# A two-layer transformer on one core: layers written out, shared splits moved, norm by halves, index keys and forget columns from row products, last expert step tile by tile

## The chip, the cores and the metric

The kernel runs on one core of a Trainium2 chip. The metric is the device time of one execution in microseconds, the median of several runs. Engines: PE (TensorE matmul; PEld is its weight load), DVE (VectorE), ACT (ScalarE), POOL (GpSimd) and SP (SyncE), which only issues DMAs here.

## The reference, cut to what matters

Two layers, 256 tokens (two tiles of 128), width 1024, float32.

```
for layer in range(2):
    fox_qkv, fox_f, dsa_qkv, idx_q, idx_k, idx_w, c_q, c_kv, k_r, band_qkv = split(x @ w_in[layer])
    mixed = concat([fox_group(fox_qkv, fox_f, b_forget[layer]),     # decay = cumsum(log_sigmoid(f + b))
                    dsa_group(dsa_qkv, idx_q, idx_k, idx_w, t5),     # keeps the 64 best keys by index score
                    mla_group(c_q, c_kv, k_r, ...),                  # rms_norm of c_q, c_kv, then w_uq, w_ukv
                    band_group(band_qkv, chunk_rel_bias[layer])])
    x = layer_norm(ALPHA * x + mixed @ w_out[layer])
    scores = sigmoid(x @ w_router); sel = top_k(scores + bias, 8)
    ffn = sum over 64 experts e of gate[e] * (silu(x @ gu[e]) * ...) @ down[e]  +  shared expert
    x = layer_norm(ALPHA * x + ffn)
```

The index score is `sum_h relu(iq_h . ik) * iw_h`: 8 heads of 32 against one key of 32.

## The kernel before, in words

A weight enters a ring `raw` of six slots by a DMA of SP, about 1 MB a piece. Exact float32 products are made of three fp32r products: ACT casts the weight to a high part, POOL (in the first half of a layer) or DVE (later) subtracts to get the low part, and PE adds `xh*wh + xl*wh + xh*wl`. The order on each engine is written out by hand, and semaphores join the engines. One loop over the layers (`Fori(0, DEPTH)`, lines 498, 630, 709, 1119 and 1455) runs on every engine; in it lies a loop of 15 passes over the experts and a 16th pass written apart (`step(NIT - 1, True)`).

Stages of a layer, with the names that the change touches:

- **Projection.** `transpose_x` turns x, ACT and DVE split it (L1130, L1459). Then PE runs jobs 0 to 13, each a product with one unit of `w_in` (48 matmuls of 256 columns; L694). Job 0 is the index query. Job 1 (`columns(job(1)[0:IDM...])`, line 737) makes the index key transposed, 24 matmuls with only 32 stationary columns, and ACT copies it into four bands of `ik_t` (L1205). Job 2 makes index key, index weight and `c_q` by rows. `index_dots(1)` follows, ACT applies relu (`relus(1)`, L1161), and DVE runs `index_scores(1)` (L1475, L1478), which frees the way for `mark_top` (L1488, L1490: rounds of max and replace) and for the scaling of the latents `c_q` and `c_kv` (L1510, L1511). PE meanwhile runs jobs 3, 4 and 5; job 5 (line 743) is 24 matmuls with 4 stationary columns for the forget logits. Then PE waits for `latent_ready` (line 747), transposes the latents (L749 to L751), runs job 6 and the small products L758 to L769.
- **Attention.** For each group and tile: `query_key`, `biased_max` on DVE, `exps` on ACT, `normalize` on DVE (L1590), `transpose_probs` on PE (L797), `values` (L810). Jobs 7 to 13 and the output product (`out_part`, L826) fill PE between them. Between `biased_max("fox", 0)` and `normalize("fox", 0)` DVE does `mark_top(0, 4)` and `keep_top(0)` (L1488 to L1495).
- **Norm 1.** After `mixed_low("dsa", 1)` DVE makes the low parts of both halves of the shared expert's weight (`shared_lo`, L1633) and then runs `layer_norm` for tile 0 and tile 1 (L1437 to L1451). ACT makes their high parts (`shared_hi`, L1318) after `mixed_high("dsa", 1)`.
- **Router.** PE transposes x (L679), runs quarter 0 of the shared gate and up product (L910 to L912), the router product (L956), four matmuls with zeros that open the output banks (L960), quarters 1 to 3 between the small products that rank the experts, and then the shared down product (L933), which needs `a_hi`, `a_lo` from DVE (L1710, L1701, L1703). These need the silu of the shared gate (`silu_dense(0)`, L1353), which stands behind the copies of the first rows on ACT.
- **Experts.** Each pass takes a dense expert A, a gathered one B and a pair C1, C2. The end of a pass: B down (L1059), A down (`dense_down`, L933), scatter of B (L947), pair down (L1085), scatter of C (L947). In the 16th pass `tile0_done` and `moe_done` rise once a tile, after the last scatter into it.
- **Norm 2.** `layer_norm` on the whole tile of 1024 columns: one add of the residual (L1437), two `bn_stats` (L1441), then the rest. `x_next` starts the next layer.

SP reloads the ring for the next layer (L515) as the 16th pass frees the slots: slots 0, 1 and 2 first, then 3, 4, 5.

## Time and profile before

| what | us |
|---|---|
| median of 3 runs (lowest, highest) | 1816.24 (1814.83, 1820.38) |
| the profiled execution: its own time | 1813.22 |
| the profiled execution: its span | 1811.4 |
| PE busy | 1712.4 (95%) |
| DVE, ACT, POOL busy | 986.2, 768.0, 227.4 |
| mean granted clock | 0.977 |
| DMA | 509.26 MB, mean 281 GB/s |

The span is one execution of the program; its own time is the device time of the same execution. A busy PE is not PE at its peak, since matmuls overlap: a row of one matmul shows 0.28 us where the next begins 0.12 us later. Times in the rows count from the span's start. Layer 0 lies at 0 to 906, layer 1 at 906 to 1811; what one row shows for layer 1 stands in layer 0 about 890.9 us earlier.

### The profile page before, as it was taken

How to read it: one execution, taken by the hardware profiler on the slowest of the kernel's cores; microseconds unless marked ns; L12 is line 12 of the kernel's file. 1: busy time of each engine (PE TensorE's matmuls, PEld its weight loads, DVE VectorE, ACT ScalarE, POOL GpSimd, SP SyncE). 2: the span in 40 equal slices, each digit the busy share in tenths (PEclk: the TensorE clock that was granted, in tenths of full speed). 3: DMA queues.
4: the chain of work that ended last, by engine and by line, in shares of the span. 5: the costliest groups of instructions: out<-in, count | busy, mean ns of one | idle time of the engine just before them, and what ended most of it. 6: DMA issues, size and time to landing. Idle time of an engine off the chain costs nothing.

```text
span 1811.4 us, 29520 instructions
## 1 busy us (share of the span) xinstructions
PE 1712.4 (95%) x10302; PEld 1302.3 (72%) x10302; DVE 986.2 (54%) x1441; ACT 768.0 (42%) x1020; POOL 227.4 (13%) x160
## 2 busy tenths in 40 slices
PE   7798999999999999999979988999999999999996
PEld 6687766777777777767677876777776777777774
DVE  2746455555555555555457555555555555555554
ACT  4464333443444434444346634443444444334331
POOL 6380000000000000000144700000000000000000
PEclk8898999999999999999989989999999999999998
DMA  8232699889899989888853228888888898888983
GB/s 286 85 130 65 222 337 328 331 332 333 334 338 332 335 333 335 333 330 320 290 173 114 97 70 325 330 334 336 336 332 335 317 327 336 330 322 334 330 322 116
DMA packets 136091, 509.26 MB, mean 281 GB/s; under 512 B 11588, under 2 KB 50920, under 8 KB 102760
## 3 DMA queue, kind: packets, MB, share of 16 engines
q1 hardware_dynamic: 122288, 467.77, 70.0%
q0 software_dynamic: 9792, 35.66, 6.0%
q10 hardware_dynamic: 3960, 5.17, 0.9%
q8 instruction: 30, 0.49, 0.1%
q14 instruction: 21, 0.17, 0.0%
HBM read 505.14 MB, written 3.41 MB: 281 GB/s over the span
## 4 chain that ended last, share of the span: by engine, by line
PE 81%; DVE 7%; DMA 4%; ACT 3%; DVEq 2%; issue 2%; ACTq 0%; SPq 0%; PEldq 0%
PE ps L1044 11%; PE ps L933 10%; PE ps L1018 10%; PE ps L910 7%; PE ps L947 7%; PE ps L911 7%; PE ps L912 7%; PE ps L1085 6%; PE ps L694 5%; PE ps L1059 5%; DMA raw<-in_w_exp_down_dram 2%; PE ps L940 2%; PE ps L826 1%; DVE o_lo L1745 1%; DMA raw<-in_w_exp_gu_dram 1%
## 5 line engine op out<-in xcount | busy, mean ns | idle before, releaser
L1717 DVE TENSOR_TENSOR raw_r<-raw,w_hi 128x2048 fp32r<-128x2048 f32 x192 | 439.9, 2292 | 397.6 <-ACT w_hi L1365 397.6
L1365 ACT CAST w_hi<-raw 128x2048 fp32r<-128x2048 f32 x192 | 365.7, 1906 | 286.7 <-DMA raw<-in_w_exp_down_dram 175.5
L910 PE MATMUL ps<-x_hi,w_hi 128*128 128x256 f32 x1088 | 311.4, 286 | 1.8 <-DVE x_lo L1643 1.8
L911 PE MATMUL ps<-x_lo,w_hi 128*128 128x256 f32 x1088 | 306.9, 282 | 0.0
L912 PE MATMUL ps<-x_hi,raw_r 128*128 128x256 f32 x1088 | 306.2, 281 | 0.0
L1044 PE MATMUL ps<-raw,xc 128*64 128x512 f32 x1024 | 233.8, 598 | 0.0
L910 PEld LDWEIGHTS ps<-x_hi,w_hi 128*128 128x128 f32 x1088 | 206.6, 190 | 31.4 <-issue 30.1
L911 PEld LDWEIGHTS ps<-x_lo,w_hi 128*128 128x128 f32 x1088 | 207.9, 191 | 1.5
L912 PEld LDWEIGHTS ps<-x_hi,raw_r 128*128 128x128 f32 x1088 | 206.7, 190 | 0.0
L657 POOL DMA_INDIRECT xg_b<-x_by_token,token_b x32 | 30.1, 940 | 1248.2 <-DVE token_c L1696 1248.2
L1044 PEld LDWEIGHTS ps<-raw,xc 128*64 128x64 f32 x1024 | 67.8, 136 | 119.4 <-issue 115.0
L1745 DVE TENSOR_TENSOR o_lo<-ps,o_hi 128x512 fp32r<-128x512 f32 x128 | 87.8, 688 | 58.2 <-ACT o_hi L1415 24.3
L933 PE MATMUL ps<-w_hi,a_hi 128*128 128x512 f32 x272 | 112.2, 413 | 6.3 <-DVE a_lo L1703 6.3
L1085 PE MATMUL ps<-raw,at_c 128*64 128x512 f32 x512 | 116.9, 598 | 0.0
L933 PE MATMUL ps<-w_hi,a_lo 128*128 128x512 f32 x272 | 107.9, 397 | 0.0
L1018 PE MATMUL ps<-w_hi,xb_hi 128*128 128x512 f32 x256 | 102.5, 401 | 1.3 <-DVE xb_lo L1725 1.3
L933 PE MATMUL ps<-raw_r,a_hi 128*128 128x512 f32 x256 | 101.0, 395 | 0.0
L1018 PE MATMUL ps<-raw_r,xb_hi 128*128 128x512 f32 x256 | 100.5, 392 | 0.0
L1018 PE MATMUL ps<-w_hi,xb_lo 128*128 128x512 f32 x256 | 99.8, 390 | 0.0
L1085 PEld LDWEIGHTS ps<-raw,at_c 128*64 128x64 f32 x512 | 33.9, 136 | 66.6 <-issue 66.6
L636 POOL TENSOR_TENSOR raw_r<-raw,w_hi_odd 128x1024 fp32r<-128x1024 f32 (+1 forms) x28 | 68.6, 2471 | 63.5 <-ACT w_hi_odd L1126 63.5
L694 PE MATMUL ps<-x_hi,raw_r 128*128 128x256 f32 (+2 forms) x256 | 74.9, 293 | 0.0
(314 smaller groups left out, 2962.3 us busy)
## 6 DMA issues: line engine op xcount, KB each, us to landing
raw<-in_w_exp_gu_dram SPq DMA_DIRECT2D x256, 1024.0 KB, 6.4
raw<-in_w_exp_down_dram SPq DMA_DIRECT2D x128, 1024.0 KB, 7.5
raw<-in_w_in_dram SPq DMA_DIRECT2D x22, 1024.0 KB, 5.8
raw<-in_w_out_dram SPq DMA_DIRECT2D x8, 1024.0 KB, 5.1
row_b<-gates_by_rank SPq DMA_DIRECT2D x30, 256.0 KB, 5.7
row_c<-gates_by_rank SPq DMA_DIRECT2D x60, 128.0 KB, 5.3
raw<-in_w_sh_gu_dram SPq DMA_DIRECT2D x4, 1024.0 KB, 5.4
row_a<-gates_by_rank SPq DMA_DIRECT2D x32, 128.0 KB, 8.1
```

The lines of the kernel that those rows point to most:

```text
L694: last = nc.tensor.matmul(o, a, b, start=(c == 0 and i == 0), stop=(c == KC - 1 and i == 2))
L910: nc.tensor.matmul(o, h, x_hi[:, c, :], start=(first and i == 0), stop=False, skip_group_check=True)
L911: nc.tensor.matmul(o, h, x_lo[:, c, :], start=False, stop=False, skip_group_check=True)
L912: last = nc.tensor.matmul(o, l, x_hi[:, c, :], start=False, stop=(final and i == 3), skip_group_check=True)
L933: last = nc.tensor.matmul(ps[:, 4 + 2 * t + half, :], lhs, rhs, start=False, stop=False, skip_group_check=True)
L947: last = nc.tensor.matmul(ps[:, 4 + 2 * t + half, :], place[:, t * P:(t + 1) * P], part[:, half * 512:(half + 1) * 512], start=False, stop ...
L1018: last = nc.tensor.matmul(ps[:, 2, :], a[:, c, :], b[:, i, :], start=(c == 0 and k == 0), stop=(c == KC - 1 and k == 2))
L1044: last = nc.tensor.matmul(ps[HALF * h:HALF * (h + 1), 3, :], xc[:, c, HALF * h:HALF * (h + 1)], piece_slot(j % RING, u)[:, i, :], start=(c ...
L1085: last = nc.tensor.matmul(ps[HALF * h:HALF * (h + 1), 2 + half, :], at_c[:, c, HALF * h:HALF * (h + 1)], piece_slot(j % RING, 2)[:, c, hal ...
L1365: nc.scalar.copy(w_hi[CAST[j] % 3][:], raw[:, j % RING, 0:UNIT_F]).then_inc(hi_done, 1)
L1717: nc.vector.tensor_tensor(raw_r[:, s, 0:UNIT_F], raw[:, s, 0:UNIT_F], w_hi[CAST[j] % 3][:], ALU.subtract)\
L1745: nc.vector.tensor_tensor(o_lo[:, part], ps[:, bank + half, :], o_hi[:, part], ALU.subtract)\
```

## The change

`for layer in range(DEPTH)` takes the place of all five layer loops, so each layer has its own code; the loop over the experts stays. The rest, cut to its core:

```diff
 # PE: projection. Job 1 gone, later jobs one number lower; job 5 gone
-columns(job(1)[0:IDM, 0:SEQ], layer, 1, 0, IDM, True).then_inc(job_ps, 1)
-project_rows(2, 1)
-pe.wait_ge(job_sb, done(layer, job_sb, 2))
+project_rows(1, 1)
+o = job(2)
+rows(o, layer, 2, (0,))
+pe.wait_ge(ik_rows_sb, done(layer, ik_rows_sb, 1))
+for t in range(NT):
+    last = nc.tensor.transpose(ps[:, 4, t * P:(t + 1) * P], ik_rows[:, t]..., ident[:])
+last.then_inc(ik_ps, 1)
+rows(o, layer, 2, (1,)).then_inc(job_ps, 1)
+pe.wait_ge(ik_sb, done(layer, ik_sb, 1))
 index_dots(1)
-project_rows(3, 2)
-project_rows(4, 3)
-columns(job(5)[0:NH, 0:SEQ], layer, 3, GW, NH, False).then_inc(job_ps, 1)
+tile_rows(job(3), layer, 3, 0).then_inc(job_ps, 1)      # 24 matmuls of 260 columns each
+tile_rows(job(4), layer, 3, 1).then_inc(job_ps, 1)
 ...
+    last = nc.tensor.transpose(ps[0:NH, 5, SEQ + t * P:...], f_tok[:, t, :], ident[:])   # after the latents' transposes
 # ACT: projection
-for r in range(4): last = nc.scalar.copy(ik_t[IDM * r:IDM * (r + 1), :], o[0:IDM, 0:SEQ])
+nc.scalar.copy(ik_rows[:], o[:, :, 0:IDM].unsqueeze(2).to_broadcast([P, NT, 4, IDM])).then_inc(ik_rows_sb, 1)
 split_pre(3)
 nc.scalar.mul(iw[:], ...)
-relus(1)
 nc.scalar.copy(cq_tok[:], ...)
+act.wait_ge(ik_ps, done(layer, ik_ps, 1))
+nc.scalar.copy(ik_t[:], ps[:, 4, 0:SEQ]).then_inc(ik_sb, 1)
 ... squares of cq_tok ...
 o = bank(2)                 # was bank(3)
 split_pre(4)
+relus(1)
 nc.scalar.copy(ckv_tok[:], o).then_inc(job_sb, 1)
 ...
+for t in range(NT):         # jobs 3 and 4; the root of the rms stands inside, at t == 0
+    o = bank(3 + t)
+    if t == NT - 1: split_pre(5)
+    nc.scalar.copy(v_tok["fox"][:, t, :], o[:, 0:GW])
+    nc.scalar.copy(f_tok[:, t, :], o[:, GW:GW + NH]).then_inc(job_sb, 1)
+    if t == 0: wait var_ready; Sqrt of rms
 relus(0)
 # DVE: attention and norm 1
 biased_max("fox", 0)
-mark_top(0, 4)
-keep_top(0)
-normalize("fox", 0)
+mark_top(0, 2)
+normalize("fox", 0)
+mark_top(0, 2)
+keep_top(0)
 ...
 mixed_low("dsa", 0)
+shared_lo(0)
 mixed_low("dsa", 1)
-shared_lo(0); shared_lo(1); layer_norm(tile 0); layer_norm(tile 1)
+layer_norm(tile 0); shared_lo(1); layer_norm(tile 1)
 # ACT: shared_hi(0) before probs_out("dsa", 1), shared_hi(1) after it, both before mixed_high("dsa", 1);
 # silu_dense(0) right after the copies of mask_t, waiting for shared_gate_ps (quarter 1 done)
 # PE: the four matmuls with zeros from before quarter 1 to behind the matmul that makes ranked_ps
 def layer_norm(layer, t, bank, signal, roots, ready):
+    for half, (s, n) in enumerate(ready):
+        dve.wait_ge(s, n)
+        scalar_tensor_tensor(part, part, ALPHA, ps[:, bank + half, :], mult, add)
+        dve.drain()
+        bn_stats(stats[:, t, half, :], part)
 # PE: the 16th pass, behind B down and the transposes of a_c
+pair_down()
+add_b()
+for t in range(NT):
+    for half in range(2):
+        last = dense_down(t, *weights(AD), (half,))
+        if t == 0 and half == 0: pe.wait_ge(c_out_sb, ...)
+        scatter(place_c, t, (half,)).then_inc((tile0_done, moe_done)[t], 1)
 # ACT, 16th pass: waits for b_added before it reads C's output
 # SP: before a layer's load into slot k it waits for the last use in the order (0, 1, 2, 4, 5, 3)
```

## Rows read from the trace of the kernel before

**Rows 1.** The profile's page, part 1: busy time, share of the span, instructions.
```profile
PE 1712.4 (95%) x10302; PEld 1302.3 (72%) x10302; DVE 986.2 (54%) x1441; ACT 768.0 (42%) x1020; POOL 227.4 (13%) x160
```

**Rows 2.** Busy time by stage: stretch, length, engines' busy us, granted clock, DMA share, GB/s.
```profile
219.80:886.00 666.20, 657.95 (x3728) 478.58 (x3728) 365.37 (x478) 271.68 (x291) 28.10 (x30) 1.00 0.89 330
886.00:919.30 33.30, 22.41 (x98) 14.42 (x94) 18.13 (x27) 8.48 (x14) 6.72 (x4) 0.83 0.73 238
```

**Rows 3.** Waits of PE, whole span: us in total, times, longest us.
```profile
PE ps L679 <- DVE x_tok L1451: 23.3, 6, 5.0
PE ps L749 <- DVE ckv_tok L1511: 9.4, 2, 8.7
PE ps L797 <- DVE probs L1590: 7.7, 4, 3.0
```

**Rows 4.** Timeline of ACT, layer 1: start us, us, engine, line, operation.
```profile
936.45 2.02 ACT L1126 CAST w_hi_odd<-raw 128x1040 fp32r<-128x1040 f32 x2 [4.22 <-PE ps L694]
938.45 2.04 ACT L1161 ACTIVATE ps<-ps 128x512 f32<-128x512 f32 x4
943.48 2.00 ACT L1126 CAST w_hi_even<-raw 128x1024 fp32r<-128x1024 f32 x2 [1.51 <-PE ps L694]
```

**Rows 5.** Timeline of DVE at the latents' scaling, layers 0 and 1.
```profile
55.24 1.89 DVE L1510 TENSOR_SCALAR cq_tok<-cq_tok,rms 128x192 f32<-128x192 f32 x1
57.05 2.36 DVE L1511 TENSOR_SCALAR ckv_tok<-ckv_tok,rms 128x128 f32<-128x128 f32 x1
...
952.25 0.32 DVE L1510 TENSOR_SCALAR cq_tok<-cq_tok,rms 128x192 f32<-128x192 f32 x1
```

**Rows 6.** Chain that ended last, layers 0 and 1: start us, us, piece.
```profile
61.44 7.42 PE ps L694 x48
...
919.33 17.10 PE ps L694 x120
...
954.12 5.63 PE ps L694 x48
```

**Rows 7.** Timelines of POOL, DVE and ACT, layer 1, around fox.
```profile
981.75 5.13 POOL L636 TENSOR_TENSOR raw_r<-raw,w_hi_even 128x1024 fp32r<-128x1024 f32 x2 [4.38 <-ACT w_hi_even L1126]
...
981.91 2.73 DVE L1590 TENSOR_TENSOR probs<-probs,row_inv 128x512 f32<-128x512 f32 x1
...
990.41 1.16 ACT L1268 COPY mk_t<-ps 32x256 f32<-32x256 f32 x4
```

**Rows 8.** Timeline of DVE, layer 1, before norm 1.
```profile
1051.63 4.50 DVE L1633 TENSOR_TENSOR raw_r<-raw,w_hi 128x2048 fp32r<-128x2048 f32 x2 [1.38 <-ACT w_hi L1318]
1056.04 1.22 DVE L1437 SCALAR_TENSOR_TENSOR x_tok<-x_tok,ps 128x1024 f32<-128x1024 f32 x1
```

**Rows 9.** Timelines of PE and ACT, layer 1, the router.
```profile
1079.04 1.17 PE L960 MATMUL ps<-x_hi,zeros 128*128 128x512 f32 x4
...
1092.52 1.28 ACT L1353 ACT_TABLE_LOAD   x1 [0.61 <-PE ps L912]
1093.82 0.60 ACT L1353 ACTIVATE silu<-ps 128x512 f32<-128x512 f32 x1
...
1096.61 0.79 PE L933 MATMUL ps<-w_hi,a_hi 128*128 128x512 f32 x1 [3.19 <-DVE a_lo L1703]
```

**Rows 10.** Timelines of PE and DVE at layer 0's end.
```profile
898.74 3.65 PE L1085 MATMUL ps<-raw,at_c 128*64 128x512 f32 x16
903.92 0.47 PE L947 MATMUL ps<-o_hi,place_c 128*128 128x512 f32 x1 [1.53 <-DVE o_lo L1745]
...
905.20 1.22 DVE L1437 SCALAR_TENSOR_TENSOR x_tok<-x_tok,ps 128x1024 f32<-128x1024 f32 x1 [1.43 <-PE ps L947]
...
915.26 1.28 DVE L1451 SCALAR_TENSOR_TENSOR x_tok<-x_tok,rstd,ln_b 128x1024 f32<-128x1024 f32 x1
```

**Rows 11.** Line 709 (the layer loop) on PE's queue; ACT's timeline at the boundary.
```profile
L709 PEldq COMPARE_BRANCH  x2: 74/2994/5913, 904.0 to 1794.5; - x2
...
916.60 1.28 ACT L1130 ACT_TABLE_LOAD   x1 [2.44 <-issue]
```

More of the change, by code:

```diff
@@ L629, in _ @@
                                pattern=[[-1, NH], [0, P]], channel_multiplier=1).then_inc(consts_built, 1)
-            with pool.Fori(0, DEPTH) as layer:
+            for layer in range(DEPTH):
                 def split_lo(k, before):
@@ L882, in _ @@
                 values("mla", 0)
[L883 removed]
+                pe.wait_ge(job_sb, done(layer, job_sb, 13))
                 out_part(0, FOX_C + BAND_C, (2, 3), first=True)
@@ L941, in gathered_t, with scatter @@
                     last.then_inc(signal, 1)
-                def scatter(place, t):
-                    for half in range(2):
+                def scatter(place, t, halves=range(2)):
+                    for half in halves:
                         for part in (o_hi, o_lo):
@@ L958, in _ @@
                 last.then_inc(router_ps, 1)
-                for b in range(2 * NT):
-                    nc.tensor.matmul(ps[:, 4 + b, :], zeros[:], x_hi[:, 0:2, :], start=True, stop=False, skip_group_check=True)
                 shared_gate_up(1)
@@ L1102, in step @@
-                    if not final:
+                        pe.wait_ge(place_c_ready, done(layer, place_c_ready, it + 1))
+                        pe.wait_ge(c_out_sb, done(layer, c_out_sb, it * 2 + 2))
+                        for t in range(NT):
+                            scatter(place_c, t)
                         pe.wait_ge(xb_lo_sb, done(layer, xb_lo_sb, it * 2 + 4))
@@ L1118, in _ @@
             act.dma_start(t5_dram, t5_row[:]).then_inc(t5_stored, 16)
-            with act.Fori(0, DEPTH) as layer:
+            for layer in range(DEPTH):
                 def split_pre(k, halves=range(2)):
@@ L1334, in _, with silu_dense @@
                     .then_inc(scores_ready, 1)
+                def silu_dense(n):
+                    act.wait_ge(a_ready, done(layer, a_ready, n))
+                    nc.scalar.activation(silu[:].rearrange("p c t -> p (c t)"), ps[:, 0, :], ACT.Silu).then_inc(silu_a_done, 1)
                 shared_hi(2)
@@ L1454, in _ @@
                 dve.sem_inc(s, START[s])
-            with dve.Fori(0, DEPTH) as layer:
+            for layer in range(DEPTH):
                 for b in range(4):
```

267 lines of the change are left out of this document (139 added, 128 removed).

## The prediction

> **What bounds the kernel now.** I read the page's busy times first: PE is busy for 95% of the span [rows 1]. That is an average, so I went to the busy times by stage. In the expert passes PE works 657.95 of 666.20 us at granted clock 1.00, DVE and ACT about half of that, and the DMA engines are 0.89 busy [rows 2]. The change leaves the 15 looped passes as they are, so 30 of the 32 passes should not move. In the 33.3 us around the layer boundary PE is busy 22.41 us only, at clock 0.83 [rows 2]: there and between the attention and the first pass the time can change. The waits of PE say on whom: on the second norm result (L679, 23.3 us in six waits), on the scaled latents (L749: 9.4 us in two, of which one is 8.7, so the other is 0.7), and on the normalized probabilities (L797: 7.7 us in four, the longest 3.0) [rows 3]. The chain of waits and the engines' timelines give the rest. I price one layer at a time, since the two latents' waits are so different.
>
> **Index keys and forget columns by rows.** What goes: 24 matmuls of job 1 and 24 of job 5. The chain has 120 matmuls in 17.10 us, of which 28 ran at the half rate; the 48 of a later job take 5.63 us, 0.117 us each [rows 6]. So 2.8 + 2.8 = 5.6 us of PE work go from each layer. In their place stand two transposes for the keys and two for the forget columns, about 0.1 us each (0.2 at the half clock), and 4 more columns on 48 matmuls (1.6% of 5.6 us, 0.1). The question is whether PE could use the gain. PE waits for `latent_ready`, and that hangs on this chain: relu of the index dots on ACT, index scores, six rounds of max and replace, scaling, all on DVE.
>
> In layer 1 the chain gets longer at its head. Before, `relus(1)` ran at 938.45, right behind the cast of unit 3 [rows 4], when 120 matmuls had ended. Now job 1 by rows (48) and job 2 (48) stand before the dots, so it is 144 matmuls: 2.8 us later, with the transposes 3.1. And `relus(1)` stands behind `split_pre(4)`, which waits for job 2 and takes 2.00 us where the cast of unit 3 took as much [rows 4]. PE's job 0 ends at 927.8; plus 5.6, 2.8, 0.3, 2.8 gives 939.4 for the end of job 2; plus 2.0 for the cast gives 941.4 against 938.45. So all that follows on DVE is 2.9 us late.
>
> Then comes a second loss. In layer 0 the scaling ran while POOL split unit 5: 1.89 and 2.36 us where the same operation takes 0.32 in layer 1 [rows 5]. Layer 1 escaped because ACT waited for job 5 (until 951.8) before it cast unit 5, and POOL began at 953.0, behind the first scalings. Job 5 is gone, so ACT casts unit 5 as soon as it has the root, as in layer 0. I take layer 0's stretch: the four scalings take 4.6 us from the first's start (55.24 to 59.8) instead of 0.95, less 0.4 because the cast no longer waits for a copy: +3.3. `latent_ready` comes at 953.2 + 2.9 + 3.3 = 959.4, and PE, done with its jobs at about 949, idles 10 us.
>
> Third: behind layer 0's idle of 8.7 us, 48 matmuls took 7.42 us, behind layer 1's 0.7 us 5.63 [rows 3, 6]: +1.8. The transposes before them also run at the half rate: +0.7, and +0.4 for the two new ones. Sum for layer 1: 2.9 + 3.3 + 1.8 + 0.7 + 0.4 = **+9.1 us**. Bounds: 2.2 if the hold and the clock fall away and ACT overlaps something, 10.5 if the hold is layer 0's in full.
>
> In layer 0 the head has slack: DVE is held until 43.5 by the bias tables, and the later `relus(1)` would end at 42.1. The 0.4 us that the hold loses pay the two new transposes: **0** (0 to +1.5). The forget logits now come behind the latents; the decay is then ready near 972 in layer 1, and PE wants it after job 6, near 980: nothing.
>
> The Trainium skill, "SBUF — State Buffer", section "SBUF: two separate sides", calls the port pair that VectorE and GpSimd share an exclusive lock, held for a whole instruction, that bites VectorE operations with two SBUF inputs or in a two-port mode. By that rule the hold comes wherever POOL's split is under way; without it this part would be near +5.
>
> **Rounds after the normalization.** PE waits 3.0 us a layer at L797, for a `normalize` of 2.73 us that began 0.2 us after POOL's split did [rows 3, 7]. Put two rounds of max earlier it starts near 980.1 and ends at 980.8, before POOL's 981.75: PE's wait is gone. But what is late next? `keep_top` falls into POOL's split now and is held till its first half ends (984.2), so `biased_max("fox", 1)` gains only 0.4; ACT's `exps("fox", 1)` follows it, and the copies to `mk_t`, which PE awaits, end at 991.6 now [rows 7], 0.3 before PE reads them. So PE waits there instead: **-0.6 us a layer** (0 to -3.0; I stay at the near end, as ACT's order is fixed).
>
> **Shared splits and norm 1.** Before, 4.50 us of low parts stood before the first norm, which began at 1056.04 [rows 8], though its product had ended at 1048.3. Now DVE is free at 1050.25 (after `mixed_low`). A norm takes 5.7 us (1056.04 to 1061.7); by halves it costs one more start on each of two operations, +0.3. So 1050.3 + 6.0, then 2.25 for the second low part, then 6.0: 1064.6 against 1067.4. DVE binds, not PE's product (ended 1058.2). ACT's two casts of 1.9 us lie in gaps before the probabilities' copies; the first low part lies before `mixed_low("dsa", 1)`, in an idle stretch of 5.3 us. **-2.75 us a layer** (-1.5 to -3.5).
>
> **Router.** The four zero matmuls go from a place where PE was the bound to one where it idled 3.19 us [rows 9]: -0.95, their start to start. `silu_dense(0)` had its table load of 1.28 and its 0.60 us on the way to `gated` [rows 9]; now DVE goes on as soon as its `tokens` end (1093.1), a further -1.3. The idle before L933 shrinks from 3.19 to about 0.9, less the zeros; the first six of its matmuls ran at the half rate (0.43 us apart, not 0.23), so up to -1.2 more. Against this the gathered rows and the DMAs behind `ranked_stored` come only about 1.1 and 1.8 us earlier. The silu's new wait for quarter 1 (ended by 1083) holds the copies of `by_expert` behind it on ACT, but they await PE until 1087 anyway. I take **-2.7 us a layer** (-1.5 to -4).
>
> The Trainium skill, "ScalarE: Activation LUTs", section "What ACT_TABLE_LOAD costs", gives some 2.66 us for a switch with its drain. The row has 1.28, and the silu starts right behind it at 1093.82. By the page this part would be -4.1; the trace decides.
>
> **16th pass and norm 2.** `pair_down` comes first. It needs `at_c`, ready at 892.04, so it starts at 892.15, 0.8 us idle after 891.36. With 3.63 for it, 1.86 for B's scatter: 897.65. ACT and DVE then need 2.2 us for C's output, half hidden by 1.4 us of dense down; tile 0's first half is complete at 900.5, the second at 902.3, and the statistics end near 903.8, where they ended at 907.8: tile 0's norm ends at 907.0. Tile 1 is complete at 906.0, DVE binds: 907.0 + 6.0 = 913.0 against 916.5 (915.26 + 1.28) [rows 10]. **-3.55 us a layer** (-2 to -4.5). Behind ACT's new wait for B's scatter stand only C's copies, and DVE's `o_lo` waits for those. PE's 1.53 us wait for `o_lo` [rows 10] is replaced by one of about 0.9. Queues: SP now asks for slot 3 only after the last down product and for 4 and 5 behind it, at about 906 instead of 897 to 903; three loads of 3.2 us end near 916, and ACT first wants unit 3 at 930.
>
> **Layers written out.** PE's branch back took 5.9 us (904.0 to 910.0) [rows 11], hidden behind the norm of tile 0 that ended at 910.9. With tile 0 at 907.0 it would delay only its transposes, so the jump is worth little by itself. ACT had its branch and a table load of 1.28 us on the path of `x_hi` [rows 11]; layer 1's middle, which has none, goes from the norm to the first low part 0.5 us faster: **-0.5, once**. Register operations before waits go too: under 1 us, taken as 0. In the looped passes a wait still needs a register: 0 (bounds below).
>
> **Sum.** 9.1 - 2 x (0.6 + 2.75 + 2.7 + 3.55) - 0.5 = 9.1 - 19.2 - 0.5 = -10.6 us. On the profiled execution's 1813.2 us that is 1802.6. The median shown is 3.0 us above that execution, so I state 1805.6.
>
> **Rivals.**
> 1. *The latents cost little.* Layer 1's late head is absorbed, the hold and the half clock don't come: +2.2 instead of +9.1, so 1816.2 - 17.5 = 1798.7, or less if the earlier normalization reaches PE in full (-4.8): 1794. For it: POOL's start moves with ACT's, and 0.7 us were enough to escape. Against: layer 0 shows hold and clock under just this order.
> 2. *The gains at the norms stay small.* `pair_down` waits for its last piece, issued at 884.8 and landed near 889.8, 2.3 us before the need; and DVE's norm in halves takes longer. Half of the 19.2 us and the full +9.1: -1, so 1815.
> 3. *Slower: the looped passes get longer.* A pass is 43.1 us and the 30 looped passes are untouched in text, but they now exist twice, in a longer program. If the code behind the loop's branch has to be fetched again, as at the layer's branch (5.9 us for PE [rows 11]), even a tenth of that, 0.6 us a pass, is +18: 1816.2 - 10.6 + 18 = 1823.6. It decides from 0.35 us a pass on. Against: PE is idle for only 8 of 666 us in the passes, the inner branch included [rows 2].
>
> **How the numbers follow.** Forecast 0.50 (its own range 1801 to 1811), rival 1 0.28, rival 2 0.12, rival 3 0.10. What a measurement here can tell from no change is 0.3%, 5.4 us. Faster by more: 0.47 of the forecast, all of rival 1 and 0.02 of rival 2, 0.77; within: 0.03, 0.10 and 0.02, 0.15; slower: 0.08. The range for 8 in 10 runs from rival 1's low end to the near side of rival 2: 1794 to 1813.
>
> **What would show it.** In the profile after, per step: PE's wait at the latents' transposes in layer 1 (some 10 us for 0.7), the scalings of `cq_tok` there at about 2 us and the job behind them at 7.4; a `normalize("fox", 0)` of 0.7 us and a new PE wait for ACT's `mk_t`; norm 1 starting right after `mixed_low`; no PE wait over 1.5 us before the shared down product; the last norm 3.5 us sooner after B's down product. The prediction is wrong if layer 1's latents are ready within 3 us of their old place, or if a looped pass is not 43.1 us.

## The result, and the profile after

The changed kernel takes 1803.4 us in the median of six runs (1800.4 to 1805.7), the kernel before 1815.5 (1810.1 to 1820.5, six). The ratio is 0.9928, 95% interval 0.9907 to 0.995: faster by 9 to 17 us, by medians 12.1. Forecast were 1805.6 us and 10.6 us less. The profiled execution has a span of 1801.6 us, against 1811.4.

Some words used below. A split is the subtraction that makes the low part of a weight; on POOL it comes in two halves of some 2.4 us each. A hold is the time by which a DVE operation is longer beside a split. Half rate is TensorE at the lower of its two clocks.

I cut both traces at the same matmuls: the first projection, the latents' transposes (L749, now L766), the query matmuls (L758, L779), the probabilities of fox 1 (L797, L818), the first output matmul, the first shared one (L910, L931), the first of B's in a pass (L1018, L1041). Each number is the difference of two start times, in us; only the row from the last output matmul counts from its end.

```
layer, stretch                         before   after  difference  forecast
0  first projection -> latents          43.01   44.46     +1.4        0
0  latents -> query matmuls              8.80    8.71     -0.1        0
0  query matmuls -> fox 1               32.31   31.96     -0.4       -0.6
0  fox 1 -> first output matmul         34.86   36.93     +2.1        0
0  last output matmul -> shared         12.16    9.03     -3.1       -2.75
0  shared -> first expert matmul        35.82   31.10     -4.7       -2.7
0  first pass                           43.96   44.42     +0.5        0
0  14 looped passes                    604.4   604.0      -0.5        0
0  last pass -> layer 1's projection    55.74   51.96     -3.8       -3.55 and -0.5
1  first projection -> latents          33.92   37.90     +4.0       +6.2
1  latents -> query matmuls              6.35    8.84     +2.5       +2.9
1  query matmuls -> fox 1               32.32   31.68     -0.6       -0.6
1  fox 1 -> first output matmul         34.85   34.62     -0.2        0
1  last output matmul -> shared         12.17    9.04     -3.1       -2.75
1  shared -> first expert matmul        35.83   32.70     -3.1       -2.7
1  first pass                           44.39   46.89     +2.5        0
1  14 looped passes                    603.5   604.4      +0.9        0
1  last pass -> end                     57.37   53.75     -3.6       -3.55
```

(The output product itself is 0.15 shorter in each layer.) The page's busy times answer to [rows 1]: 88 matmuls fewer, the share unchanged.

```profile
PE 1703.4 (95%) x10214; PEld 1292.6 (72%) x10214; DVE 989.6 (55%) x1449; ACT 763.3 (42%) x1019; POOL 226.3 (13%) x160
```

By stage, as in [rows 2] (length, then busy us of PE, PEld, DVE, ACT, POOL, granted clock, DMA share, GB/s): layer 0's looped passes; the last pass with the boundary; and in layer 1 the latents, the job behind them, and on to fox 1.

```profile
253.00:859.00 606.00, 599.63 (x3375) 435.45 (x3374) 334.07 (x436) 249.60 (x268) 26.28 (x28) 1.00 0.90 331
859.00:910.58 51.58, 43.91 (x240) 31.29 (x239) 28.27 (x41) 13.94 (x21) 6.80 (x4) 0.95 0.76 257
910.58:948.49 37.91, 26.44 (x227) 25.34 (x227) 22.93 (x46) 17.87 (x39) 24.29 (x10) 0.86 0.65 198
948.49:957.33 8.84, 8.84 (x57) 8.59 (x58) 5.80 (x19) 5.29 (x9) 0.00 (x0) 0.72 0.00 0
957.33:989.01 31.68, 28.89 (x207) 24.41 (x205) 20.65 (x61) 17.62 (x41) 14.13 (x6) 1.00 0.34 107
```

The passes are as full as before: a looped pass is 43.14 to 43.17 us against 43.11 to 43.17. In layer 1's third row PE works 26.4 of 37.9 us, and behind it, at clock 0.72, it is busy all the time and slow. The waits of PE answer to [rows 3]:

```profile
PE ps L766 <- DVE ckv_tok L1555: 20.1, 2, 10.3
PE ps L687 <- DVE x_tok L1495: 16.6, 4, 5.3
PE ps L741 <- DVE drop L1522: 5.1, 2, 4.2
PE ps L818 <- ACT mk_t L1319: 4.6, 2, 2.5
PE ps L818 <- DVE probs L1634: 1.9, 3, 0.9
```

The norms' wait (L679, now L687) lost 6.7 us, the latents' (L749, now L766) gained 10.7; the fox probabilities' went from 7.7 to 1.9, and `mk_t` took their place with 4.6. New is also a wait of 5.1 us in two for the index scores to be read (L741): 4.2 in layer 0, 0.9 in layer 1.

### The profile page after: what moved, and what is told of

The parts are those of the page before. It is cut to its first block, busy times and chain, and to the rows that moved or that the text cites. A ratio compares the mean times of both kernels' runs of the same rounds, so it can differ in the third digit from the quotient of the medians.

```text
span 1801.6 us, 28743 instructions
## 1 busy us (share of the span) xinstructions
PE 1703.4 (95%) x10214; PEld 1292.6 (72%) x10214; DVE 989.6 (55%) x1449; ACT 763.3 (42%) x1019; POOL 226.3 (13%) x160
## 4 chain that ended last, share of the span: by engine, by line
PE 80%; DVE 8%; DMA 5%; ACT 3%; issue 2%; DVEq 2%; ACTq 0%; SPq 0%; PEldq 0%; POOLq 0%
PE ps L1067 11%; PE ps L1041 10%; PE ps L956 9%; PE ps L931 7%; PE ps L970 7%; PE ps L932 7%; PE ps L933 7%; PE ps L1107 6%; PE ps L1082 5%; PE ps L702 4%; DMA raw<-in_w_exp_down_dram 2%; PE ps L963 2%; DVE o_lo L1790 1%; PE ps L847 1%; ACT o_hi L1458 1%
## 5 line engine op out<-in xcount | busy, mean ns | idle before, releaser
L931 PE MATMUL ps<-x_hi,w_hi 128*128 128x256 f32 x1088 | 311.1, 286 | 1.8 <-DVE x_lo L1687 1.8
L931 PEld LDWEIGHTS ps<-x_hi,w_hi 128*128 128x128 f32 x1088 | 206.1, 189 | 31.3 <-issue 30.1
L665 POOL DMA_INDIRECT xg_b<-x_by_token,token_b x32 | 30.5, 952 | 1243.2 <-DVE token_c L1740 1243.2
L1041 PE MATMUL ps<-w_hi,xb_hi 128*128 128x512 f32 x256 | 102.6, 401 | 0.4 <-DVE xb_lo L1770 0.4
L1041 PE MATMUL ps<-raw_r,xb_hi 128*128 128x512 f32 x256 | 100.4, 392 | 0.0
L1041 PE MATMUL ps<-w_hi,xb_lo 128*128 128x512 f32 x256 | 99.8, 390 | 0.0
L1433 ACT ACTIVATE silu_b<-ps 128x256 f32<-128x256 f32 x32 | 12.4, 387 | 140.7 <-PE ps L1041 140.7
```

Source lines behind the costliest of these rows:

```text
L931: nc.tensor.matmul(o, h, x_hi[:, c, :], start=(first and i == 0), stop=False, skip_group_check=True)
L1041: last = nc.tensor.matmul(ps[:, 2, :], a[:, c, :], b[:, i, :], start=(c == 0 and k == 0), stop=(c == KC - 1 and k == 2))
```

## Experiments

Each kernel was timed in rounds with the kernel before on its chip; ratios are to that kernel.

**u_idx**: the changed kernel, with the index keys and the forget columns as column jobs again.

```diff
-                project_rows(1, 1)
-                o = job(2)
...
+                columns(job(1)[0:IDM, 0:SEQ], layer, 1, 0, IDM, True).then_inc(job_ps, 1)
+                project_rows(2, 1)
...
-                tile_rows(job(3), layer, 3, 0).then_inc(job_ps, 1)
-                tile_rows(job(4), layer, 3, 1).then_inc(job_ps, 1)
+                project_rows(3, 2)
+                project_rows(4, 3)
+                columns(job(5)[0:NH, 0:SEQ], layer, 3, GW, NH, False).then_inc(job_ps, 1)
```

> The changed kernel (1803.4 us) with the index keys and the forget columns taken back to their own column jobs (14 jobs, old relu and scaling order); all else stays changed. Theory (the latents cost in layer 1): from layer 1's first projection to the latents' transposes 37.9 us fall to about 32, and the 8.8 us from there to the query matmuls to 6.3, so some 8 us less in layer 1; in layer 0 about 1.4 less before the transposes, and if the wait for the mk_t copies with the half clock behind it hangs on the new order, 2 more behind the first probabilities. Together 1792 to 1796 us. Rival 1 of the prediction (the latents cost little, the job by rows is as good): within 2 us of 1803.4, since the 48 matmuls a layer that come back take 5.6 us of PE where the wait for the latents shrinks by as much.

1796.4 us, ratio 0.9879 (0.9837 to 0.9921). Windows of layer 1, to the latents and behind them:

```profile
919.46:951.45 31.99, 31.66 (x273) 29.77 (x273) 15.55 (x45) 16.46 (x34) 19.11 (x8) 0.96 0.66 202
951.45:957.79 6.34, 6.34 (x55) 6.34 (x56) 3.77 (x10) 6.25 (x14) 4.81 (x2) 1.00 0.53 168
```

PE has more matmuls (273 records for 227) and is through 5.9 us earlier, since it idles for 0.3 us and not for 11.5, and the clock behind it is 1.00. The theory holds for these stretches (8.4 us less in layer 1, 1.6 in layer 0), and rival 1 of the prediction falls. The price of the part, 7 us, is by medians only: four executions lie between 1790.3 and 1808.2, and the interval meets that of the changed kernel at its edge (0.9921 against 0.9907).

The trace is of the slowest of the four, 1808.2 us, and shows where some 8 of its us went. In layer 0 DVE's normalization for band takes 10.84 us, where the same operation takes 0.69, PE waits 8.9 us for it, and the stretch from fox 1 to the first output matmul is 44.8 us (36.9 in the changed kernel):

```profile
114.61 10.84 DVE L1616 TENSOR_TENSOR probs<-probs,row_inv 128x512 f32<-128x512 f32 x1
...
115.63 4.68 POOL L642 TENSOR_TENSOR raw_r<-raw,w_hi_out 128x1024 fp32r<-128x1024 f32 x2
120.24 4.66 POOL L642 TENSOR_TENSOR raw_r<-raw,w_hi_odd 128x1024 fp32r<-128x1024 f32 x2
```

It begins beside a split that started at 110.90 and ends at 125.45, behind the last of the splits that follow without a pause. No other kernel here has a normalization over 3.3 us.

**u_tail, u_norm1, u_router**: the changed kernel with one of the three other parts undone.

```diff
                     if final:
-                        pair_down()
-                        add_b()
                         pe.wait_ge(split_done, cast(layer, split_done, it, AD))
...
-                    layer_norm(layer, t, 4 + 2 * t, x_next, 4 + t, [(s, done(layer, s, half + 1)) for half in range(2)])
+                    layer_norm(layer, t, 4 + 2 * t, x_next, 4 + t, [(s, done(layer, s, 1))] * 2)
```

(In u_tail the four parts of the last pass stand in the order of the other passes again.)

```diff
-                shared_lo(0)
                 mixed_low("dsa", 1)
+                for u in range(2):
+                    shared_lo(u)
```

(u_norm1; ACT's `shared_hi` is behind `mixed_high("dsa", 1)` again, and the norm waits for a whole tile.)

```diff
                 last.then_inc(router_ps, 1)
+                for b in range(2 * NT):
+                    nc.tensor.matmul(ps[:, 4 + b, :], zeros[:], x_hi[:, 0:2, :], start=True, stop=False, skip_group_check=True)
                 shared_gate_up(1)
```

(u_router; `silu_dense(0)` is behind the copies of `row_b` and `row_c` again.)

> The changed kernel with the old order of the 16th pass (dense down, B's scatter, pair_down, C's scatter) and the second norm waiting for a whole tile. Theory: the last pass up to the next layer's first projection gets 3.6 to 3.8 us longer in each layer (52.0 back to 55.7, 53.8 back to 57.4), and the boundary's half-clock stretch, 17.0 us before and 6.8 us after, comes back and adds up to 1.8 in the first job: 1810.5 to 1812.5 us. Rival (the boundary is shorter because the layer's branch and its table load are gone, not because of the order of the pass): only +1 to +3 a layer, 1806 to 1808, with the half-clock stretch still near 7 us.

> The changed kernel with the shared units' high and low parts both back ahead of the first norm, and that norm waiting for a whole tile. Theory (DVE was the bound, 4.5 us of low parts stood ahead of the norm): from the last output matmul to the first shared gate/up matmul 9.0 us go back to about 12.2 in both layers, 1809.7 us. Rival (half of the 3.1 us comes from the norm by halves alone or from fewer register operations): 10.5 us there and 1806.5.

> The changed kernel with the four zero matmuls and the first silu at their old places. The stretch from the first shared matmul to the first expert matmul shrank by 4.7 us in layer 0 and 3.1 in layer 1, but layer 1's first pass got 2.5 us longer (0.5 in layer 0). Theory A (the third piece of the first pass is bound by its DMA, so what the router gives in layer 1 is taken back by a wait and the half clock behind it): with the old order the stretch is 4.7 and 3.1 longer, and the first pass 0.5 and 2.5 shorter, 1808.2 us. Theory B (the long first pass of layer 1 is a clock event that has nothing to do with the router): the stretch grows the same, the first pass stays at 46.9, 1811 us.

u_tail: 1811.1 us, ratio 0.9977 (0.996 to 0.9994). The last pass to the next projection is 56.1 and 57.8 us (52.0 and 53.8): +4.1 twice. The gain is the order of the pass with the norm by halves, which this run undoes together, and not the layer's branch. The second half of the theory fails: the first job of layer 1 has only 6 matmuls at half rate, fewer than the changed kernel. u_norm1: 1810.0, ratio 0.9967 (0.9945 to 0.999), 12.7 us from the output to the shared product in both layers (9.0), as the bound of DVE has it (12.2 before, plus 0.24 for each of two norms by halves). Its DVE, layer 1:

```profile
1058.76 4.49 DVE L1678 TENSOR_TENSOR raw_r<-raw,w_hi 128x2048 fp32r<-128x2048 f32 x2 [1.38 <-ACT w_hi L1359]
1063.16 0.68 DVE L1483 SCALAR_TENSOR_TENSOR x_tok<-x_tok,ps 128x512 f32<-128x512 f32 x1
```

u_router: 1807.9, ratio 0.9951 (0.993 to 0.9972), which overlaps that of the changed kernel, so that the 4.5 us are by medians. The stretch grew to 35.8 and 35.3 us, but layer 1's first pass stayed long, 46.8: my theory A (the gain is taken back there) is wrong as stated. Theory B has the first pass right (46.9), but the stretch grew by 4.7 and 2.6 only, and 1811 was not reached. The first pass was 43.9 to 47.8 us over all kernels here, whatever order the router had; ACT waits some 7.6 us for the first down piece in both profiles, which is a lead and not a cause shown. ACT's cast of it, layer 1, in the changed kernel:

```profile
1116.27 1.91 ACT L1406 CAST w_hi<-raw 128x2048 fp32r<-128x2048 f32 x1 [7.67 <-DMA raw<-in_w_exp_down_dram]
```

and in u_router:

```profile
1121.85 1.91 ACT L1404 CAST w_hi<-raw 128x2048 fp32r<-128x2048 f32 x1 [7.52 <-DMA raw<-in_w_exp_down_dram]
```

Stretch and first pass together are 79.8 to 82.1 us in the six layers with the old router and 75.5 to 80.4 in the 22 with the new one. What of the spread is the DMA's and what is the clock's stays open.

**only_loop**: the kernel before, with the layers written out and nothing else (on SP one line that served its loop, `lower_ap_dma`, goes too).

```diff
-            with pe.Fori(0, DEPTH) as layer:
+            for layer in range(DEPTH):
```

(The same on each of the five engines.)

> The kernel before with the two layers written out, nothing else (the loop over the passes stays). Theory (the branch and the table load of ACT are all that goes): 0.5 us less on the path at the layer boundary, up to 2 if the half-clock stretch there shortens; a looped pass stays at 43.1 to 43.2 us: 1813.5 to 1815.5. Rival 3 of the prediction (the longer program makes the loop's branch dearer): passes of 43.5 us or more, 1826 or more. Rival (the branch was most of the boundary's gain): the last pass up to the first projection of layer 1 falls from 55.7 to 53 or less, 1812.5.

1810.05 us (10 runs), ratio 0.9967 (0.9955 to 0.9978): 6.5 us less, where every expectation had 0.5 to 3. The looped passes didn't lengthen (43.29 and 43.11 us), so rival 3 of the prediction falls. The last pass to the projection is 55.3 for 55.7: the 0.5 of the boundary is right. Another 2.9 came in the attention: 30.9 and 30.9 us from the query matmuls to fox 1, for 32.3 and 32.3. DVE and POOL in layer 1:

```profile
978.88 0.69 DVE L1589 TENSOR_TENSOR probs<-probs,row_inv 128x512 f32<-128x512 f32 x1
...
980.64 4.76 POOL L635 TENSOR_TENSOR raw_r<-raw,w_hi_even 128x1024 fp32r<-128x1024 f32 x2 [6.02 <-ACT w_hi_even L1125]
```

Before, this normalization began at 981.91 and POOL's split at 981.75 [rows 7], so it was late by 0.16 us and held for 2.0. Counted from the first query matmul of fox, that is 7.87 us; now it is 7.52, in both layers, and 7.70 would have been early enough. DVE's small pauses ahead of a wait (0.25 and 0.17 us by its timeline, "issue") are gone; that the loop's registers made them fits, but no row names them. In this trace another thing helps: PE's job ahead (48 matmuls) ran partly at half rate, 7.48 us for 5.90, so ACT's cast and POOL's split came 1.7 us later than before, and even the old normalization would have been ahead. That the 0.35 us are enough alone is shown by u_max below. Another 2.0 and 1.5 us lie ahead of the latents, and there TensorE's rate differs: of the first job's matmuls 13 and 16 were spaced 0.21 us (half rate), for 30 and 28 before, and the others 0.12. Whether the edit brings that or this execution had it, one profile doesn't tell. The profiled execution as a whole is 3.7 us shorter, since the first pass and the looped passes of layer 0 are 1.8 and 1.6 longer; of the 6.5 us by medians only the 2.9 around fox and the 0.5 of the boundary have a place that is shown.

**u_max**: the changed kernel, with `normalize("fox", 0)` behind all four rounds and `keep_top(0)`. **keep_late**: the changed kernel, with `keep_top(0)` moved behind the normalization of fox 1.

```diff
-                mark_top(0, 2)
-                normalize("fox", 0)
-                mark_top(0, 2)
+                mark_top(0, 4)
                 keep_top(0)
+                normalize("fox", 0)
```

```diff
-                keep_top(0)
                 biased_max("fox", 1)
                 normalize("fox", 1)
+                keep_top(0)
```

> The changed kernel with normalize(fox,0) back behind all four rounds of max and keep_top(0). Theory of the prediction (the early normalization takes 3.0 us of PE's wait away and 2.1 to 2.5 come back at mk_t): the stretch from the query matmuls to fox 1's transposes goes from 31.7 to 32.3 in layer 1, 0.6 us a layer, 1804.6 us. Rival (the held normalization and the held keep_top are two forms of one wait on POOL's split, and without it the old order is the better by what keep_top loses): 0 to 1 us less, 1802.4 to 1803.4.

> The changed kernel with keep_top(0) behind normalize(fox,1), nothing else. Theory (keep_top, held by POOL for 1.8 us, delays the maximum of fox 1, ACT's exponentials and with them the copies to mk_t that PE awaits): PE's wait of 2.5 and 2.1 us for mk_t falls to under 1 us, the stretch from the query matmuls to the transposes of fox 1 goes from 32.0 and 31.7 to about 30.3, and layer 0's half clock stretch behind the wait goes: 1799 to 1801 us. Rival (POOL's lock then falls on biased_max(fox,1) or on normalize(fox,1) instead, which take as long): nothing, 1803.4.

u_max: 1797.0 us (five runs, 1796.6 to 1808.7), ratio 0.9924 (0.9897 to 0.9951): the interval doesn't part it from the changed kernel, but the trace does. Layer 1's window to fox 1, then the timelines of DVE and POOL with the normalization and the split:

```profile
955.36:985.40 30.04, 28.79 (x206) 24.43 (x205) 18.79 (x61) 17.59 (x40) 14.44 (x6) 1.00 0.34 106
```

```profile
977.41 0.69 DVE L1634 TENSOR_TENSOR probs<-probs,row_inv 128x512 f32<-128x512 f32 x1
...
977.67 5.05 POOL L644 TENSOR_TENSOR raw_r<-raw,w_hi_even 128x1024 fp32r<-128x1024 f32 x2 [4.54 <-ACT w_hi_even L1164]
```

The expectation and its rival (1802.4 to 1804.6) both missed it. With the layers written out the old order escapes POOL by itself, by 0.26 us (0.18 in layer 0), and is 1.6 to 1.9 us shorter than the new one, which puts `keep_top` under the split.

That price hangs on the rate of PE's job ahead. Six layers of the kernels with the new order here have that job in 5.9 to 6.0 us; the split then starts 22.3 us behind the query matmuls, `keep_top` takes 2.0 us, and the stretch is 31.6 to 32.0. In five others (u_router, lat_first, layer 0 of u_tail) the job took 7.4 to 7.5 us, the split starts at 23.8, `keep_top` takes 0.23, and the stretch is 30.8 to 30.9, as in only_loop with the old order. So the slower job gives the shorter stretch, and as far as these traces go the orders differ only where the job runs at full rate. (Layer 1 of u_idx and split5_late stand apart with 34.4 to 34.9: DVE was held earlier there, at the scan.)

keep_late has the early normalization and a `keep_top` behind the split: 1798.5 us, ratio 0.9902 (0.9882 to 0.9922), the stretch 29.9 and 29.6 us, and PE's wait for `mk_t` 0.5 and 0. Its theory holds.

**lat_first**: the changed kernel, with sums, root and scalings of the latents behind one round of max instead of six. The last two rounds and `keep_top(1)` go behind the decay scan. **lat_keep**: lat_first and keep_late together.

```diff
                 index_scores(1)
-                mark_top(1, 4)
                 dve.wait_ge(sums_ready, done(layer, sums_ready, 1))
...
-                mark_top(1, 2)
+                mark_top(1, 1)
                 dve.wait_ge(root_ready, done(layer, root_ready, 1))
...
                 last.then_inc(latent_ready, 1)
+                mark_top(1, 3)
                 index_scores(0)
...
-                keep_top(1)
                 dve.wait_ge(f_log_ready, done(layer, f_log_ready, 1))
                 nc.vector.tensor_tensor_scan(decay[:], f_abs[:], f_neg[:], 0.0, ALU.add, ALU.subtract).then_inc(decay_ready, 1)
+                mark_top(1, 2)
+                keep_top(1)
```

> The changed kernel with the latents' sums, root and scalings moved ahead: behind one round of max instead of six (the other rounds follow: three before index_scores(0), two before the decay scan, two behind it). Theory (the cost of the new order in both layers is that PE waits for the scaling and then runs at half clock): in layer 1 the index scores end at 937.6 and the scalings would end near 940 instead of 948.4, right behind PE's last index dots (938.2), so PE's wait of 10.3 us falls to about 2 and the half clock behind it (2.5 us) goes; in layer 0 the wait of 9.8 falls to about 2 likewise. Start to latents 36.5 and 30 us (44.5 and 37.9), latents to query matmuls 6.4 (8.7 and 8.8): 20 us less, near 1783. Rival A (DVE is the bound a step later: the rounds only move, and rope, fox bias and the first maxima come late by what PE gains): PE waits some 5 us a layer before the fox probabilities, gain 8 to 10, near 1794. Rival B (POOL's split of unit 5 holds the scalings or the rounds wherever they are): the latents come 3.3 later than above, near 1790.

> As the one with the latents ahead, and keep_top(0) behind normalize(fox,1) as well. Theory: the two waits are apart, so both gains add: PE's wait for the copies to mk_t (2.1 to 2.5 us a layer) falls by the 1.8 us that POOL holds keep_top, so 2 to 4 us under the kernel with the latents ahead alone. Rival: with PE earlier, DVE is late everywhere before the fox maxima and keep_top is no longer under POOL's split: within 1 us of the other.

lat_first: 1792.9 us, ratio 0.9874 (0.9855 to 0.9892): half of what its theory said. PE's wait fell from 9.8 and 10.3 to 5.5 and 6.1 us only. lat_keep: 1789.2, ratio 0.9852 (0.9834 to 0.987), 3.7 less again, as said by number. The step isn't shown: in lat_first's profile both layers have the slower job, `keep_top(0)` is not held (0.23 us) and PE doesn't wait for `mk_t` at all. DVE and POOL of lat_keep, layer 1:

```profile
933.40 2.47 DVE L1553 TENSOR_SCALAR cq_tok<-cq_tok,rms 128x192 f32<-128x192 f32 x1
935.79 2.36 DVE L1554 TENSOR_SCALAR ckv_tok<-ckv_tok,rms 128x128 f32<-128x128 f32 x1
...
933.41 4.66 POOL L644 TENSOR_TENSOR raw_r<-raw,w_hi_odd 128x1024 fp32r<-128x1024 f32 x2 [4.01 <-ACT w_hi_odd L1164]
```

The same root releases ACT's cast, ACT's first half releases POOL, and POOL starts 0.01 us behind the first scaling: 4.8 us for the two operations instead of 0.6. That is rival B, and most of the missing half: with the hold gone (best, below) the two waits are 1.3 and 1.8 us.

**split5_late**: the changed kernel, with ACT's cast of unit 5 behind the forget gates' `f_z`, so that POOL starts on it later. **best**: that and lat_keep. **best2**: lat_keep, with the cast right behind `relus(0)`.

```diff
                     o = bank(3 + t)
-                    if t == NT - 1:
-                        split_pre(5)
...
                 nc.scalar.activation(f_z[:], o, ACT.Identity, bias=b_f[:]).then_inc(f_read, 1)
+                split_pre(5)
```

(split5_late and best.)

```diff
                 relus(0)
+                split_pre(5)
                 act.wait_ge(latent_ps, done(layer, latent_ps, 1))
```

(best2.)

> The changed kernel with ACT's cast of unit 5 moved from ahead of the second copy of the forget job to behind the forget gates' first two operations (before their exponential), so that POOL's low part of unit 5 starts after the latents are scaled. Theory (POOL's split holds the first two scalings for 3.3 us): the scalings of cq_tok and ckv_tok take 0.32 and 0.28 us instead of 1.4 and 2.4, the latents are ready 3.0 to 3.3 us earlier in layer 1 (37.9 to 34.7) and 3.5 to 4.0 earlier in layer 0 (44.5 to 40.8), and PE's two waits of 9.8 and 10.3 us shrink by as much; the half clock behind them stays: 1796 to 1798 us. Rival A (project_t(6) or ACT's own chain is late by the move): the stretch from the query matmuls grows by 2 us a layer, 1801. Rival B (the long scalings have another cause than POOL): no change, 1803.4.

> The latents ahead, keep_top(0) behind normalize(fox,1), and ACT's cast of unit 5 behind the forget gates' first two operations. Theory: what the kernel with the first two edits (1789.2 us) still waits for at the latents is POOL's hold of 4.1 us on the scalings (2.47 and 2.36 us for 0.32 and 0.28); without it PE's waits of 5.5 and 6.1 us shrink to 1.4 and 2.0, and the half clock behind them (10.2 us stretches in both layers) shortens by one or both: 4.1 x 2 plus 1 to 3, so 1778 to 1781 us. Rival (DVE or unit 5's low part becomes late for project_t(6), which PE reaches near 945 us): gain 3 to 5 only, 1785.

> As the kernel with all three edits (1789.9 us), but ACT casts unit 5 right behind relus(0), not behind the forget gates' operations: POOL's low part would then run from about 934.5 to 939.2, beside rounds of max and index scores only, which POOL never lengthened in any run. There the low part fell on the forget gates' addition (2.25 us for 0.27) and the next one but one on two rope operations (2.22 and 2.40 for 0.22), and PE's stretch from the query matmuls to fox 1's transposes was 34.5 and 34.2 us where it is 29.6 to 30.9 without. Theory (the hold isn't lost by moving a split, it lands on DVE's next operation between two SBUF tiles; only beside rounds and PSUM operations it is free): start to latents stays at 36.6 and 29.8, the addition takes 0.27, DVE reaches the rope 2 us earlier and mostly ahead of unit 7's low part, the stretch falls to 30.5 to 32.5: 1783 to 1787 us. Rival (unit 7's low part still meets the rope, as its start hangs on PE's project_t(6) which is no later): the stretch stays over 34, 1788 to 1790.

split5_late: 1804.8 us, ratio 0.9952 (0.9936 to 0.9967), nothing gained, where theory had 1796 to 1798 and rival A 1801. The latents came 2.2 and 2.5 us earlier, and the stretch from the query matmuls to fox 1 grew by 2.9 and 2.8. best: 1789.9, ratio 0.9865 (0.9849 to 0.9882), as lat_keep, and worse than both the theory (1778 to 1781) and its rival (1785). Its DVE and POOL in layer 1 show where it went:

```profile
932.97 0.32 DVE L1552 TENSOR_SCALAR cq_tok<-cq_tok,rms 128x192 f32<-128x192 f32 x1
...
941.25 2.25 DVE L1560 TENSOR_SCALAR f_abs<-f_abs 4x256 f32<-4x256 f32 x1
...
955.64 2.22 DVE L1579 TENSOR_TENSOR mq_tok<-rope_ab 128x64 f32<-128x64 f32 x1
957.79 2.40 DVE L1581 TENSOR_TENSOR mq_tok<-rope_ab 128x64 f32<-128x64 f32 x1
...
938.57 4.78 POOL L644 TENSOR_TENSOR raw_r<-raw,w_hi_odd 128x1024 fp32r<-128x1024 f32 x2 [9.59 <-ACT w_hi_odd L1164]
...
955.17 4.94 POOL L644 TENSOR_TENSOR raw_r<-raw,w_hi_odd 128x1024 fp32r<-128x1024 f32 x2 [5.11 <-ACT w_hi_odd L1164]
```

The scalings are free (0.32 for 2.47), and the hold falls on the forget gates' addition, and by the next but one split on two rope operations that take 0.22 us elsewhere. In best2 unit 5's split runs beside the rounds of max, which it doesn't lengthen: 1783.3 us (1780.7 to 1786.8, six runs), ratio 0.9823 (0.9789 to 0.9857). It beats the changed kernel by 20 us in medians, 19 by the two ratios. Its windows of layer 1, to the latents, behind them, and to fox 1:

```profile
899.69:930.10 30.41, 27.45 (x226) 26.35 (x227) 16.41 (x30) 16.55 (x38) 19.62 (x8) 0.93 0.76 232
930.10:936.67 6.57, 6.57 (x56) 6.52 (x57) 5.52 (x19) 6.08 (x10) 4.78 (x2) 1.00 0.21 72
936.67:970.13 33.46, 30.36 (x206) 25.75 (x204) 27.87 (x77) 17.78 (x42) 14.54 (x6) 0.95 0.30 95
```

In layer 0 the last stretch is 29.9 us, in layer 1 still 33.5: there unit 7's split meets two rope operations (2.37 and 2.38 us). Layer 0 is the theory's (30.5 to 32.5) and better, layer 1 lies between it and the rival's (over 34).

## Why the prediction was right, and where it was not

Of the signs of being wrong that the prediction names, none came: layer 1's latents are 4.0 us later than in the kernel before, past the 3 us, and a looped pass is unchanged. The terms one by one:

**Index keys and forget columns** (forecast 0 and +9.1; measured +1.3 and +6.5; undone, 7.0 in all). The mechanism is the one forecast; the first of its terms, the later relus of layer 1, was sized too large. Chain and scalings in layer 1 answer to [rows 5, 6]:

```profile
910.58 15.31 PE ps L702 x120
...
950.45 7.04 PE ps L702 x48
```

```profile
944.31 1.41 DVE L1554 TENSOR_SCALAR cq_tok<-cq_tok,rms 128x192 f32<-128x192 f32 x1
945.65 2.36 DVE L1555 TENSOR_SCALAR ckv_tok<-ckv_tok,rms 128x128 f32<-128x128 f32 x1
```

The four scalings took 4.1 us from the first's start (944.31 to 948.4), against 0.95 forecast to become 4.6 less 0.4: the hold of 3.3 was 3.2. The job behind the wait took 7.04 for 5.63 (+1.4 for 1.8), the transposes 2.0 for 0.9. What failed is the 2.9 us of the later relus: they end 22.4 us after the first projection (932.95 - 910.58) for 21.2 before (940.49 - 919.33), +1.2, because the first 120 matmuls took 15.3 and not 17.1 us. Nine of them ran at half rate, 28 before. I had carried the boundary's clock over as it stood; the other kernels had 6 (u_tail, u_max) to 20 (u_router, best2) there, and no row says what decides it. In layer 0 I had let the head vanish behind DVE's bias tables. They were themselves held: POOL now splits unit 3 beside them, where before a split met the bias for band, ahead of them.

```profile
40.07 5.81 DVE L1511 TENSOR_TENSOR t_bias<-t_hankel,block 128x256 f32<-128x256 f32 x4
```

It was 1.42 us before, and the index scores start 2.3 us later, at 45.8.

The rule of the Trainium skill that I had put beside this part ("SBUF — State Buffer", section "SBUF: two separate sides": an exclusive lock, for a whole instruction, on VectorE operations with two SBUF inputs or in a two-port mode) agrees with these rows: additions, scalings and the scan were held (0.27 to 2.25, 0.32 to 2.47, 0.67 to 2.29 us); rounds of max and index scores out of PSUM, beside the same splits, kept their 0.43 and 0.48. It does not explain u_idx's 10.84 us: there DVE was held over more than four of POOL's subtractions and not over one, and why it was not let in between them stays open. Without the hold the prediction has this part near +5; its own terms give 9.1 - 3.3 = 5.8.

**Rounds after the normalization** (forecast -0.6 a layer). The stretch did get 0.4 and 0.6 shorter, and what I had named took its place, in layer 1 as in layer 0 [rows 7]:

```profile
977.71 0.69 DVE L1634 TENSOR_TENSOR probs<-probs,row_inv 128x512 f32<-128x512 f32 x1
...
980.09 2.03 DVE L1539 TENSOR_SCALAR drop<-drop 128x128 f32<-128x128 f32 x1
...
987.80 1.16 ACT L1319 COPY mk_t<-ps 32x256 f32<-32x256 f32 x4
```

So the number was met by luck, for the credit is wrong. u_max shows that the written-out layers had already freed the normalization, by 0.35 us of DVE's time; on top of them the moved rounds cost 1.6 to 1.9 us a layer in this stretch, where PE's job ahead runs at full rate. And in layer 0 the wait of 2.5 us has a price that I had left out: the job behind `mk_t` took 7.48 us, at a granted clock of 0.78, where layer 1's took 6.02.

```profile
103.59:111.07 7.48, 7.48 (x52) 7.35 (x52) 0.42 (x1) 3.98 (x7) 7.48 (x4) 0.78 0.03 10
```

**Layers written out** (forecast -0.5, alone -6.5). The step that failed is "register operations before waits: under 1 us, taken as 0". As busy time they are that little. But DVE is 0.35 us sooner at the normalization, which before was 0.16 us behind the split, and u_max shows that this is enough to go first; the stretch to fox 1 is 1.4 to 1.5 us shorter in each layer of only_loop. What makes up the rest of the 6.5 us stays open.

**Norm 1** (forecast -2.75, measured -3.1 in both layers; undone 6.6 in all). DVE binds as said; answers to [rows 8]:

```profile
1046.96 0.68 DVE L1483 SCALAR_TENSOR_TENSOR x_tok<-x_tok,ps 128x512 f32<-128x512 f32 x1
...
1052.82 2.28 DVE L1650 TENSOR_TENSOR raw_r<-raw,w_hi 128x2048 fp32r<-128x2048 f32 x1
...
1059.70 1.28 DVE L1495 SCALAR_TENSOR_TENSOR x_tok<-x_tok,rstd,ln_b 128x1024 f32<-128x1024 f32 x1
```

A norm by halves costs what was forecast: from 1055.02 to 1060.98 is 5.96 us, tile 0's 5.94, where I had 6.0 and the whole one 5.7. The gain is the low part that no longer stands ahead of tile 0's norm.

**Router** (forecast -2.7 a layer; undone 4.5 in all, 2.3 a layer). The stretch itself gained 4.7 and 3.1. The zeros now stand in what is left of the idle time [rows 9], and the table load is ahead of the rows' copies:

```profile
1086.19 1.20 PE L1016 MATMUL ps<-x_hi,zeros 128*128 128x512 f32 x4
1087.91 0.51 PE L956 MATMUL ps<-w_hi,a_hi 128*128 128x512 f32 x1 [0.52 <-DVE a_lo L1747]
```

```profile
1077.31 1.28 ACT L1380 ACT_TABLE_LOAD   x1
1078.60 0.60 ACT L1380 ACTIVATE silu<-ps 128x512 f32<-128x512 f32 x1
1080.19 0.54 ACT L1391 COPY by_expert<-ps 64x128 f32<-64x128 f32 x2 [0.99 <-PE ps L997]
```

Not in the forecast was a longer first pass: PE's wait ahead of B's down product is 2.1 us in layer 1, 1.2 before, and the product behind it took 4.6 us for 3.0. It is not the price of an earlier start, since u_router, with the old order, has a wait of 2.0 us there; its cause stays open. By the Trainium skill's figure for a table switch ("ScalarE: Activation LUTs", section "What ACT_TABLE_LOAD costs") the part was to be -4.1; the undone one lies below both, nearer to the row. In the profile after, too, the load takes 1.28 us and the silu starts 0.01 us behind it.

**16th pass and norm 2** (forecast -3.55 a layer; measured -3.8 with the layer's branch, and -3.6; undone 7.7 in all). Forecast was tile 0's norm until 907.0 on the clock of before, and 913.0 for tile 1. With the 5 us by which layer 0 is early, they would be 902.0 and 908.0; they are 902.1 and 908.3, answering to [rows 10]:

```profile
900.81 1.28 DVE L1495 SCALAR_TENSOR_TENSOR x_tok<-x_tok,rstd,ln_b 128x1024 f32<-128x1024 f32 x1
...
906.99 1.28 DVE L1495 SCALAR_TENSOR_TENSOR x_tok<-x_tok,rstd,ln_b 128x1024 f32<-128x1024 f32 x1
```

The branch and the table load of [rows 11] are gone from the boundary: 0.8 us after the norm's end PE has the first transposes done and ACT starts on them, at 909.05.

Put together, the total was nearer than its terms, and that is luck in part. The parts undone and done singly give +7.0, +6.4 (u_max), -6.6, -4.5, -7.7 and -6.5, which is -11.9 in sum, for -12.1 measured; each of them is uncertain by several us (the intervals are 0.0023 to 0.0084 of 1815 us wide), so that the agreement of the sum proves little. Two terms, the rounds and the loop, I had at -1.2 and -0.5. They are off by some +8 and -6 and cancel.

## What to carry to other kernels

Where two engines share a port, look at the tenths of a microsecond between the short operation and the long one: less than half a microsecond of order (0.16 late, 0.26 early) decides two microseconds of hold, and a split that is moved takes its hold along, so put it beside operations that don't need the port. When a wait sits on a chain, see first whether the chain needs what stands in it: the latents waited behind six rounds that they had no use for, and moving them was worth 10.5 us alone and 20 with the two edits around it, against 12.1 for the whole change. And price a stall with the half clock behind it.

## What was not expected of the hardware

- Tenths of a microsecond decide the hold: a normalization 0.26 us ahead of POOL takes 0.69 us (u_max), one 0.16 us behind it 2.73 [rows 7]. At 0.01 us ahead by the profile a scaling was held (lat_keep), so the edge lies between the two.
- A hold can outlast one split: 10.84 us for 0.69 in u_idx, with PE waiting 8.9 us behind it.
- Slower can be shorter: where PE's job ahead ran at half rate and took 1.5 us more, POOL's split came too late to hold `keep_top`, and the stretch was 0.7 to 1.2 us shorter.
- The half clock is no fixed tax on a stretch: behind nearly the same idle time (5.80 and 5.95 us) the first 30 matmuls of layer 0 ran at half rate in the kernel before and the first 13 in only_loop. The executions of one kernel lay 2 us apart in lat_keep (1788.1 to 1789.8) and 18 in u_idx (1790.3 to 1808.2, at a mean granted clock of 0.987 and 0.980; some 8 of the 18 are the held normalization). So a single profile can't settle a term of 2 us that a stretch like that may fall on.
